# Mixing's modulation rows stored in DRAM by layer 0's gates, and the first splits of the output product made in the gates' tail

## The reference, cut to what matters

```python
mod = (sc @ ada_w[l] + ada_b[l])            # 6 x 1024 per token kind
sh1, sc1, g1, sh2, sc2, g2 = jnp.split(mod, 6, axis=-1)
merged = g_f * (f @ w_f) + g_na * (attn @ w_na) + g_cv * (y_cv @ w_cv)
x = x + g1 * (merged @ w_o[l])              # the same for ctx, with its own modulation
h2 = modulate(rmsnorm(x, norm2_g[l]), sh2, sc2)   # rmsnorm(x) * g * (1 + sc2) + sh2
```

## Time and profile before

| what | value |
|---|---|
| median of 3 runs | 3227.41 (3226.53 to 3232.39) |
| the profiled execution, its own time | 3229.3 |
| its span in the profile | 3227.5 |
| mean granted TensorE clock | 0.983 |
| TensorE busy | 3094.2 (96%) |
| VectorE, ScalarE, GpSimd busy | 1686.2, 899.2, 848.6 |
| DMA | 495.36 MB, mean 153 GB/s |

### The profile page before, as it was taken

How to read it: one execution, slowest core, us unless ns; L and a number is a source line. 1 busy time by engine, 2 the same in 40 slices (tenths; PEclk the granted TensorE clock), 3 DMA queues, 4 the chain that set the end, 5 groups by cost and what they waited for, 6 DMA issues and landing times. The chain is left out here.

```text
span 3227.5 us, 46862 instructions
## 1 busy us (share of the span) xinstructions
PE 3094.2 (96%) x16072; PEld 2391.0 (74%) x16073; DVE 1686.2 (52%) x2469; ACT 899.2 (28%) x1711; POOL 848.6 (26%) x536
## 2 busy tenths in 40 slices
PE   7999899999999989999999999999999988999998
PEld 4887788777777776766666888788777877666665
DVE  5473377777732666423544566365222256886640
ACT  4321365111112422222222332265211132222222
POOL 0150000110111224344443023000111123766664
PEclk9999999999999989999999999999999998999999
DMA  6122342444414348756687422242111234888853
GB/s 266 56 89 76 104 130 99 133 142 140 132 50 170 105 151 280 235 161 215 235 296 242 184 78 89 76 147 69 52 44 48 69 123 180 322 328 289 284 167 84
DMA packets 157387, 495.36 MB, mean 153 GB/s; under 512 B 30498, under 2 KB 81314, under 8 KB 134436
## 3 DMA queue, kind: packets, MB, share of 16 engines
q1 hardware_dynamic: 110880, 389.73, 32.7%
q0 software_dynamic: 17568, 59.82, 8.0%
q10 hardware_dynamic: 28804, 43.98, 4.3%
HBM read 417.42 MB, written 76.39 MB: 153 GB/s over the span
## 5 line engine op out<-in xcount | busy, mean ns | idle before, releaser
L220 PE MATMUL wide<-part,part 128*128 128x512 f32 (+2 forms) x2416 | 974.1, 403 | 28.9 <-DVE part L2738 16.5
L222 PE MATMUL wide<-part,part 128*128 128x512 f32 (+2 forms) x2416 | 927.8, 384 | 0.0
L221 PE MATMUL wide<-part,part 128*128 128x512 f32 (+2 forms) x2384 | 914.2, 383 | 0.0
L220 PEld LDWEIGHTS wide<-part,part 128*128 128x128 f32 x2416 | 457.3, 189 | 141.4 <-issue 51.4
L221 PEld LDWEIGHTS wide<-part,part 128*128 128x128 f32 x2384 | 451.8, 190 | 99.5 <-issue 18.7
L222 PEld LDWEIGHTS wide<-part,part 128*128 128x128 f32 x2416 | 456.9, 189 | 91.3
L2736 DVE CAST part<-place 128x2048 fp32r<-128x2048 f32 x128 | 198.3, 1549 | 375.1 <-DMA place<-in_w 369.5
L1853 POOL TENSOR_TENSOR place<-place,place 128x512 f32 (+3 forms) x80 | 105.5, 1319 | 1062.6 <-DVE place L1817 1062.6
L2598 PE MATMUL bank<-place,place 128*128 x832 | 365.9, 593 | 3.9 <-ACT place L2692 2.7
L2738 DVE TENSOR_TENSOR part<-place,part 128x2048 fp32r<-128x2048 f32 x128 | 351.8, 2748 | 4.4
L2598 PEld LDWEIGHTS bank<-place,place 128*128 128x128 f32 x832 | 154.1, 190 | 178.5 <-issue 178.5
(11 more groups left out here) (293 smaller groups left out, 3993.1 us busy)
## 6 DMA issues: line engine op xcount, KB each, us to landing
place<-in_w SPq DMA_DIRECT2D x118, 1024.0 KB, 8.8
place<-in_w SPq DMA_DIRECT2D x35, 2048.0 KB, 9.4
place<-in_ada_w ACTq DMA_DIRECT2D x72, 512.0 KB, 3.7
place<-in_w_gates SPq DMA_DIRECT2D x32, 640.0 KB, 4.3
place<-in_bias SPq DMA_DIRECT2D x96, 192.0 KB, 3.3
place<-in_ada_w SPq DMA_DIRECT2D x6, 2048.0 KB, 17.8
place<-in_w_rows SPq DMA_DIRECT2D x6, 2048.0 KB, 15.2
place<-in_w_gates SPq DMA_DIRECT2D x16, 768.0 KB
```

The source lines that it names most:

```text
L220: pe.matmul(out, left[0], right[0], start=first, stop=False)
L221: pe.matmul(out, left[0], right[1], start=False, stop=False)
L222: return pe.matmul(out, left[1], right[0], start=False, stop=last)
```

## The change

Layer 0's gates make, between chunks 6 and 7 (`late` in `chunks`), all rows that mixing needs in both layers. `gains` on VectorE multiplies (1 + scale) by the norm's gain, as columns; `rows_out` turns them to rows with eight transposes on TensorE; VectorE copies them from PSUM; SP stores them in two small DMAs to `mod_rows` and `gain_rows` in DRAM. GpSimd's clearing of the zeros moves behind that store and so does the fill of acc. In mixing, `load_rows` loads g1, mul and add with DMAs whose source is one row of 4 KB read for all 128 partitions; the rows of the context tokens are loaded at tile 2. All broadcasts, their copies, the load of the norm rows and VectorE's scaling of mul go. In the tail of the gates' last chunk (both layers) ScalarE and VectorE split seven of the eight slices of w_o's first half (`WO_AHEAD`) and merged tile 0. In mixing VectorE subtracts all of w_o's second half before update(0,0), and waits for the constants (s_ld, now 48) ahead of update(0,1).

The diff, cut to its core (declarations and the host's tables are left out but for those named):

```diff
@@ -1574,6 +1577,7 @@
 BRANCH_KS = (2, 4, 2)
+WO_AHEAD = 7
 GATE_W_AT = (A_QK, A_R + KD * TOK, A_QK + TOK)
@@ -1619,6 +1623,9 @@
     s_pool, s_wo = sem("gpsimd_passed"), sem("w_o_loaded")
+    s_ohi, s_olo, s_m0hi, s_m0lo = sem("w_o_hi"), sem("w_o_lo"), sem("first_merged_hi"), sem("first_merged_lo")
+    wo, ohi, olo = place(A_ATT, KD, 512), part(A_ATT + 4096, KD, 512), part(A_ATT, KD, 512)
+    m0hi, m0lo = part(A_H, NT, KD, P)[:, 0], part(A_R, KD, SEQ if last else TOK)[:, :, 0:P]
     s_zero, s_fill = sem("zeros"), sem("slots_filled")
@@ -1627,7 +1634,9 @@
     mods = s["mod"][:].rearrange("p l c w -> p (l c) w")
+    gains2 = place(at + 2048 + D + 8, DEPTH, KD, 2)
     if ada:
+        s_g2n, s_rt, s_rc, s_rs = sem("gains2"), sem("mod_rows_out"), sem("mod_rows_read"), sem("mod_rows_stored")
         s_pl = [sem(f"ada_w_loaded_{b}") for b in range(2)]
@@ -1647,15 +1656,22 @@
-    def chunks(eng, body, between=None):
+    def chunks(eng, body, between=None, late=None):
...
             between()
-        for b in range(2):
-            body(KD - 2, b, b == 1, False)
+        body(KD - 2, 0, False, False)
+        if late is not None:
+            late()
+        body(KD - 2, 1, True, False)
+    def gain_rows_of():
+        return [(gains2[:, layer, :, w], 2 * layer + w) for layer, w in ((0, 0), (0, 1), (1, 0))] + \
+            [(s["mod"][:, 1, 5 * KD:6 * KD, 0], 3)]
@@ -1669,6 +1685,12 @@
                     load_gate_weights(s, sp, layer, i, q, s_w[q])
+            if ada:
+                sp.wait_ge(s_rc, 2)
+                sp.dma_start(s["mod_rows"].rearrange("l w (c p) -> c (l w) p", p=P),
+                             sums[0:2 * KD, 0].rearrange("c (m p) -> c m p", p=P)).then_inc(s_rs, 16)
+                sp.dma_start(s["gain_rows"].rearrange("m (c p) -> c m p", p=P),
+                             sums[0:KD, 1].rearrange("c (m p) -> c m p", p=P)).then_inc(s_rs, 16)
             sp.wait_ge(s_zero, 1)
@@ -1676,6 +1698,8 @@
             sp.dma_start(s["h2_rows"][TOK:TOK + P], zeros).then_inc(s_fill, 16)
+            if ada:
+                sp.wait_ge(s_rs, 32)
             sp.wait_ge(s_bm, KD * U + 2 * NS)
@@ -1720,8 +1744,18 @@
+            def rows_out():
+                pe.wait_ge(s_g2n, DEPTH)
+                pe.wait_ge(s_keep, GATE_CHUNKS + 1)
+                for n in range(2 * DEPTH):
+                    layer, w = divmod(n, 2)
+                    pe.transpose(banks[6][0:2 * KD, n * P:(n + 1) * P], s["mod"][:, layer, 2 * KD:4 * KD, w], s["ident"][:])
+                for columns, n in gain_rows_of():
+                    mm = pe.transpose(banks[7][0:KD, n * P:(n + 1) * P], columns, s["ident"][:])
+                mm.then_inc(s_rt, 1)
             keep_turning(s, pe, banks[0], 10)
-            chunks(pe, body)
+            chunks(pe, body, None, rows_out if ada else None)
@@ -1748,6 +1782,13 @@
                     act.activation(sg[m % 2][:, 0:tn], banks[2 * (n % 3)][:, 0:tn], ACT.Sigmoid).then_inc(s_sg, 1)
+                    if final and (q, span) == (2, 0):
+                        act.wait_ge(s_wo, 16)
+                        for k in range(WO_AHEAD):
+                            act.activation(ohi[:, k], wo[:, k], ACT.Copy).then_inc(s_ohi, 1)
+                    if final and (q, span) == (2, 1):
+                        act.wait_ge(s_mg, 2 + (KD - 1) * 2 * NS + NS + 1)
+                        act.activation(m0hi, MERGED[:, :, 0:P], ACT.Copy).then_inc(s_m0hi, 1)
                     if modulate and span == 0:
@@ -1818,6 +1859,13 @@
                         keep_mods(i, b, q)
+                    if final and (q, span) == (2, 0):
+                        for k in range(WO_AHEAD):
+                            dve.wait_ge(s_ohi, k + 1)
+                            dve.tensor_tensor(olo[:, k], wo[:, k], ohi[:, k].bitcast(F32), ALU.subtract).then_inc(s_olo, 1)
+                    if final and (q, span) == (2, 1):
+                        dve.wait_ge(s_m0hi, 1)
+                        dve.tensor_tensor(m0lo, MERGED[:, :, 0:P], m0hi.bitcast(F32), ALU.subtract).then_inc(s_m0lo, 1)
@@ -1829,15 +1877,30 @@
                                       ALU.subtract).then_inc(s_slo, 1)
-            chunks(dve, body)
+            def gains():
+                dve.wait_ge(s_keep, GATE_CHUNKS + 1)
+                for layer in range(DEPTH):
+                    at = V_N2 + layer * KD
+                    dve.scalar_tensor_tensor(gains2[:, layer], s["mod"][:, layer, 4 * KD:5 * KD, :], 1.0,
+                                             s["vec"][:, at:at + KD].unsqueeze(2).broadcast_to([P, KD, 2]),
+                                             ALU.add, ALU.mult).then_inc(s_g2n, 1)
+            def rows_out():
+                dve.wait_ge(s_rt, 1)
+                dve.tensor_copy(sums[0:2 * KD, 0], banks[6][0:2 * KD, :]).then_inc(s_rc, 1)
+                dve.tensor_copy(sums[0:KD, 1], banks[7][0:KD, :]).then_inc(s_rc, 1)
+            chunks(dve, body, gains if ada else None, rows_out if ada else None)
+            dve.wait_ge(s_olo, WO_AHEAD)
+            dve.wait_ge(s_m0lo, 1)
             if ada:
-                dve.wait_ge(s_keep, GATE_CHUNKS + 1)
+                dve.wait_ge(s_rc, 2)
...
                 if ada:
-                    pool.wait_ge(s_keep, GATE_CHUNKS + 1)
+                    pool.wait_ge(s_rs, 32)
                 pool.memset(zeros, 0.0).then_inc(s_zero, 1)
@@ -1853,7 +1916,7 @@
             pool.sem_inc(s_mg, 2)
-            chunks(pool, body, clear)
+            chunks(pool, body, None, clear)
             pool.wait_ge(s_mg, 2 + KD * NS * 2)
@@ -1956,12 +2015,19 @@
+            def load_rows(w):
+                row = s["mod_rows"][layer, w:w + 1]
+                sp.dma_start(g1[:, w], row[:, 0:D].broadcast_to([P, D])).then_inc(s_g1[w], 16)
+                sp.dma_start(mul[:, w], s["gain_rows"][2 * layer + w:2 * layer + w + 1].broadcast_to([P, D]))\
+                    .then_inc(s_rows[w], 16)
+                sp.dma_start(add[:, w], row[:, D:2 * D].broadcast_to([P, D])).then_inc(s_rows[w], 16)
             load_x(0)
...
                 sp.dma_start(wo[1][:, rows], s["a"]["w_o"][layer, 1, :, rows]).then_inc(s_w[i], 16)
+            load_rows(0)
             load_x(1)
-            sp.dma_start(n2, s["a"]["norm2_rows"][layer]).then_inc(s_ld, 16)
             load_x(2)
@@ -1984,6 +2050,8 @@
                     load_x(t + 3)
+                if t == 2 and not last:
+                    load_rows(1)
                 if t == 6:
@@ -1999,16 +2067,6 @@
         def _(pe):
-            def broadcast(n):
-                v, w, h = broadcasts[n]
-                if v == 1:
-                    pe.wait_ge(s_sh, 1)
-                if n >= 4:
-                    pe.wait_ge(s_bc, n - 3)
-                src = (mod[:, layer, 2 * KD:3 * KD, :], sc2, mod[:, layer, CB:CB + KD, :])[v]
-                broadcast_columns(s, pe, [src[:, 4 * h + j, w:w + 1] for j in range(4)], banks[4 + n % 4])\
-                    .then_inc(s_b, 1)
             def product(t, h, turned=None):
@@ -2026,9 +2084,7 @@
                 pe.wait_ge(s_h2, t + 1)
-                if t == 0:
-                    pe.wait_ge(s_bc, len(broadcasts))
-                else:
+                if t:
                     pe.wait_ge(s_tc, 2 * t)
@@ -2041,7 +2097,7 @@
                 if t == 0:
-                    pe.wait_ge(s_ld, 64)
+                    pe.wait_ge(s_ld, 48)
                 pe.wait_ge(s_tc, 2 * t + 2)
@@ -2075,12 +2131,8 @@
-            for n in range(2 * NW):
-                broadcast(n)
             product(0, 0)
             product(1, 0)
-            for n in range(2 * NW, 6 * NW):
-                broadcast(n)
             product(0, 1)
@@ -2174,18 +2226,11 @@
-            def copy_rows(n):
-                v, w, h = broadcasts[n]
-                act.wait_ge(s_b, n + 1)
-                act.activation((g1, mul, add)[v][:, w, h * 512:(h + 1) * 512], banks[4 + n % 4][:], ACT.Copy)\
-                    .then_inc(s_bc, 1)
-            round_merged(0)
-            for k in range(KD):
+            act.sem_inc(s_mhi, 1)
+            act.sem_inc(s_whi, WO_AHEAD)
+            for k in range(WO_AHEAD, KD):
                 round_weights(0, k)
             round_merged(1)
-            for n in range(6 * NW):
-                copy_rows(n)
             for k in range(KD):
@@ -2223,6 +2268,7 @@
                 dve.wait_ge(s_mm, n + 1)
+                dve.wait_ge(s_g1[t // NTX], 16)
                 if n >= 2:
@@ -2234,6 +2280,7 @@
                 dve.wait_ge(s_rt, t + 1)
+                dve.wait_ge(s_rows[w], 32)
                 dve.reciprocal(rstd[:, t:t + 1], root[:, t:t + 1]).then_inc(s_r, 1)
@@ -2318,23 +2365,17 @@
-            dve.tensor_scalar(sc2, mod[:, layer, CM:CM + KD, :], 1.0, None, ALU.add).then_inc(s_sh, 1)
             dve.memset(ones, 1.0).then_inc(s_one, 1)
...
             dve.wait_ge(s_zero, 1)
+            dve.sem_inc(s_wlo, WO_AHEAD)
+            for k in range(WO_AHEAD, KD):
+                leave_weights(0, k)
```

(21 more changed lines are left out.)

9 lines of the change are left out of this document (3 added, 6 removed).

## The result

The median after is 3200.11 us (five runs, 3199.78 to 3210.71), against 3227.41 for five runs of the kernel before: a ratio of 0.9923, 95% interval 0.9911 to 0.9934, which is 21.3 to 28.7 us less. The forecast was 3207, range 3200 to 3214, faster; the median lies 0.1 inside the lower end of that range. The profiled execution took 3207.08 with a span of 3205.3, so it lies 7 us over the median of its own runs; stage by stage it can be read, as a whole it can't.

The account below looks back on a forecast made before the run. TensorE was taken as the bound, busy 3094.2 of 3227.5 us, so time comes only from its waits or removable work. 12.9 + 8.5 - 0.9 = 20.5 us off the 3227.4 median gave 3207, range 3200 to 3214.

Parts of the forecast that it names:

- the signs that I had put down: Right: tables in by 16 us; wrong: VectorE idle ahead of update(0, 1) for a DMA, or burst under 300 GB/s.
- Part 1: Head of mixing, layer 0: broadcasts go, products start 0.45 us into the stage, turn(0) comes 12.9 us earlier.
- (b): Layer 0's head: three row loads delay the tables 2.5 us, leaving 3.0 us of slack before turn(0) is late.
- The clock term: Heads of mixing: clock still falls, now under a product; 3.4 us at half speed cost 1.7 us.
- Rival D: Clock in mixing: no fall, 3.4 us less, 3203; low for 6.8 us in both layers, 3210; inside the forecast's 0.74.
- Part 2: Head of mixing, layer 1: same gain with half the broadcasts and a later start, turn(0) 8.5 us earlier.
- part 4: Splits in the gates' tail: layer 1's stage ends 0 to 1.3 us later, taken as 1.0; layer 0 covers it.
- Part 3: rows_out in layer 0's gates: eight transposes on TensorE between chunks 6 and 7 cost 0.9 us; the rest hides.
- rival E: Gates' tail: splits come late with w_o 3 us later, both layers end about 2 us later, 3211; inside forecast's 0.74.
- A: Row loads far below queue rate, 128 pieces reading the same 4 KB; at 70 GB/s 11.4 us slower, 3238; chance 0.06.
- B: Row loads at a third of the queue's rate, 140 GB/s: 4.6 us per layer, 3216; chance 0.10.
- C: Gain taken back behind turn(0) by a transfer or wait at its own time; half back is 3217; chance 0.10.

Follow-up runs that it names:

- the copies: Changed kernel with the latent tokens' rows copied 128 times within DRAM, so mixing loads each partition's row from its own address: 3200.17 us, one run.
- the wait moved: Changed kernel with VectorE's wait for the tables moved from ahead of update(0, 1) to their first use, ahead of mark_groups: 3200.9 us, ratio 0.9912.
- the version with fillers in the tail: Changed kernel with twelve small matmuls on the identity keeping TensorE busy at the end of layer 1's gates: 3204.23 us, one run.

## Why the forecast was right, and which terms were off

The direction, the mechanism and the range held, the range by luck in part: the first median, 3200.11, is 0.1 inside it and outside my own narrower 3202 to 3211. Three of the signs that I had put down showed against me: the tables came after 16 us, VectorE idled ahead of update(0, 1) for a DMA, and the burst fell under 300 GB/s. None of them cost more than 1.2 us in a head. Point by point:

**Part 1 (12.9 us less).** Shown: two pairs of profiles give 14.2. From VectorE's start to turn(0) the terms were 26.0 us; 25.33 and 25.74 were measured. No operation of the old broadcasts is left, the first product starts 0.39 us into the stage (0.45 forecast), and nothing interrupts the four products. That the kernel before spread more than I had allowed (38.92 and 40.55, according to whether the clock fell under broadcasts or under products) makes the rest of the difference.

**(b) in it, the 3.0 us of slack, is the term that was mis-sized.** I let the tables land 15.9 us after the start; they came at 18.2 or 18.3 in layer 0 and at 17.3 or 17.6 in layer 1. The price of one further row load was right (1.26 forecast, 1.2 by doubling them). Two things that no row of before showed make the 2.4 us in layer 0. The dip of two microseconds moves some 0.35 MB less than 419 GB/s would, which is 0.8 us by my estimate. The other 1.6 lie in the tail, in which only 0.15 of the DMA engines' time is in use (about what two of the sixteen engines would give; in layer 1 the tail is shorter). The cause of neither is settled. For the dip it is not the repeated reading of one DRAM row (the copies show the same landing) and not the neighbours in the queue (it moves with the loads). The slack where the clock falls is therefore 0.4 us in layer 0 (in the kernel run again the tables landed at 1042.0 and update(0, 1) began at 1042.47) and 0.9 to 1.1 in layer 1, and none in layer 0's first profile, where 0.88 us is a real wait. The Trainium skill ("DMA: Bandwidth & Descriptors", Anatomy of one DMA) has a fit for one DMA on GpSimd's path, 2.0 us and the bytes at 436 GB/s. Carried over to a row load on SP's queue and laid end to end, that would be an estimate of 3.2 us each; the doubling shows 1.2, so in this full queue the fixed part is not paid again for each load.

**The clock term (1.7).** Mostly as forecast: it fell in layer 1's head and in layer 0's when run again (25.74 against the 24.17 of a head at full clock with the wait moved, 1.6). In the first profile it fell behind turn(0) in place of in the head, and turn(0) to the last count took 131.2 us where 128.3 to 129.7 were seen elsewhere: what the head saved there, the stretch behind it lost. Rival D's "no fall, 3.4 less" did not happen in any profile of the change itself: the fall came elsewhere.

**Part 2 (8.5).** 9.9 for the head by the profiles, and 9.2 with the later start. The head took 25.5 where the sum had 26.1 from VectorE's start, and before it was 35.4. The start was 0.7 later, not 1.0, from part 4.

**Part 3 (0.9 more).** The eight transposes, TensorE between chunks 6 and 7:

```profile
959.48 0.60 PE L1752 MATMUL bank<-ident,mod 128*16 128x128 f32 x4
959.92 0.49 PE L1754 MATMUL bank<-ident,place 128*8 128x128 f32 x3
960.25 0.27 PE L1754 MATMUL bank<-ident,mod 128*8 128x128 f32 x1
960.27 0.47 PE L223 MATMUL wide<-part,part 128*128 128x512 f32 x1
```

From 959.48 to the next product at 960.27 it is 0.79, and all profiles of the change have 0.8 us more between the first addition of these gates and mixing (458.6 to 458.7 against 457.8). The rest was hidden as argued: GpSimd's clear waited 3.10 us for the stores and began at 964.21, and nothing waited for GpSimd.

```profile
964.21 0.95 POOL L1904 MEMSET place<- 128x1024 f32 x1 [3.10 <-DMA gain_rows<-place]
```

**Part 4 (1.0 in layer 1).** The seven roundings and the next sigmoid on ScalarE in layer 0, the last addition on GpSimd in layer 1:

```profile
1009.37 3.76 ACT L1788 ACTIVATE part<-place 128x512 fp32r<-128x512 f32 x7 [2.21 <-DMA place<-in_w_o]
1013.76 0.60 ACT L1784 ACTIVATE place<-wide 128x512 f32<-128x512 f32 x1 [0.64 <-PE wide L225]
```

```profile
2570.97 2.05 POOL L1916 TENSOR_TENSOR place<-place,place 128x512 f32<-128x512 f32 x1 [5.91 <-DVE place L1858]
```

The roundings left 0.64 us idle ahead of the sigmoid, which still came on time: rival E had no ground in layer 0. The addition takes 2.05 in place of the 1.26 of the earlier trace rows, because VectorE's low half of tile 0 holds it up, 0.8 and "over 2" as forecast. From TensorE's last product to the start of mixing in layer 1 it is 3.60 us against 2.90, so 0.7.

**The sum.** 20.5 forecast. The parts as measured: 14.2 + 9.9 - 0.8 (part 3) - 0.7 (part 4) = 22.6, and the stretches behind turn(0) add 1.1 and take 1.0, 22.5. The medians say 27.3 in the first series and 21.8 in the second (3228.35 less 3206.51); the two intervals, 21.3 to 28.7 and 14.5 to 25.2, both hold 22.5. The forecast's base, the median of three runs, was sound. Where the other 5 us of the first median come from is not shown: the profiles put differences of that size into stretches whose instructions the change leaves as they are.

**Rivals.** A and B (the row loads at a fraction of the rate): refuted by the copies and by the 1.2 us per load, though their route, the wait ahead of update(0, 1), is where the loss appears once the loads are doubled. C (gain taken back behind turn(0)): the two stretches cancel to 0.1 us; a gain was taken back in the first profile of the change (layer 0, by the clock) and in the version with fillers in the tail, where 3.4 us were lost behind a head shortened by 0.4. D: above. E: not seen.

## What to carry to other kernels

When TensorE stands at the head of a stage, list what it does there that is no product and ask whether it can be made once, earlier, and loaded; the price is the queue's, 1.2 us per 512 KB here and once per burst up to 2.4 us more that no row of the old trace showed, and it is to be charged against the next wait behind those loads on each engine. A preparation that is moved ahead is worth its full time only when the work that used to cover it has gone too: the splits gave 1 to 2 us a head alone and 4 us together with the rows. After such a change the heads are within 1 us of three limits at once (the tables, the clock, the norm chain), and taking away one of them moves the loss to the next.

## What the runs showed of the hardware that I had not expected

- The row loads dip once for about two microseconds (233 and 291 GB/s beside 401 and 397) with the DMA engines 0.87 to 0.89 busy, first or last in the burst, and from 128 rows as well, there less deep in layer 0 (324) than in layer 1 (229). With three more of them the windows show no second dip, and the landing moves by 1.2 us each. Behind the burst the last 1.5 us before the tables land carry 41 to 52 GB/s in layer 0.
- After the same 2.40 us without work at the change of stage the granted clock fell 1.9 us into the stage in one execution of the kernel after (2.4 to 1.2 GHz, about 1025.6 to 1029.1) and not there in another, where it fell 26.5 us into the stage, behind a pause of 2.92 us. Keeping TensorE busy over the first pause alone left the fall to the second (from about 2599.1), so one filled pause is no saved clock; with both pauses filled and the late wait it fell in neither head.
- VectorE's addition at L2278 takes 2.29 us beside GpSimd's subtraction (2.40 us, begun 0.64 before it) and 0.69 alone,'s effect the other way round: the one that starts second waits. The Trainium skill ("SBUF — State Buffer", Who interferes with whom) says this of a VectorE instruction with two on-chip inputs beside a GpSimd one that reads; the trace agrees, 1.6 us each time, once in either head.
